# Prompt attention: the causal mask of the diagonal blocks added in PSUM by VectorE instead of by products of the unit matrix

## What the kernel computes

```python
qf = q_b.astype(f32) * (HEAD_DIM ** -0.5)
m_s = (kpos <= pos[None, None, :, None, None])          # causal
p_s = jax.nn.softmax(jnp.where(m_s, s_s, NEG_INF), axis=-1)
o_s = jnp.einsum('nhgqkl,nhqkld->nqhgd', p_s, v_g)
dlt = pos[:, None] - wpos[None, :]
m_w = (dlt >= 0) & (dlt < WINDOW) & (wpos[None, :] >= 0)  # causal for 512 rows
p_w = jax.nn.softmax(jnp.where(m_w, s_w, NEG_INF), axis=-1)
return g_b[..., 0:1] * o_c + g_b[..., 1:2] * o_s + g_b[..., 2:3] * o_w
```

## Time and profile before

| what | value |
|---|---|
| time, median of 3 runs | 797.34 us (795.62 to 798.36) |
| span of the profiled execution, first to last instruction | 795.5 us |
| TensorE busy | 762.2 us (96%) |
| VectorE busy | 379.9 us (48%) |
| ScalarE busy | 204.9 us (26%) |
| GpSimd busy | 106.8 us (13%) |
| prompt attention, about 292 to 404 us of the span | 14% of the span |

### The profile page before, as it was taken

The page is one execution under the profiler, slowest core; times in us unless marked ns, Lnnn a source line. Parts: engine busy times, 40 slices in busy tenths (PEclk is TensorE's granted clock), DMA queues, the critical chain, the costliest instruction groups (busy, mean ns, idle before and its releaser), DMA issues.

```text
span 795.5 us, 12983 instructions
## 1 busy us (share of the span) xinstructions
PE 762.2 (96%) x5070; PEld 494.9 (62%) x5070; DVE 379.9 (48%) x850; ACT 204.9 (26%) x485; POOL 106.8 (13%) x160
## 2 busy tenths in 40 slices
PE   8999999999999999889999999999999999998995
PEld 5455588777778788555566775445556564654442
DVE  3269523997232323766624378434732212214865
ACT  3011213112223354654523200134111111123223
POOL 3000006000000311334500100011111101015002
PEclk9999999999999999999999999999999999999998
DMA  9640493841440499200030279003799999996002
GB/s 324 160 126 0 112 278 139 99 133 57 140 97 17 139 233 266 94 1 1 1 120 2 96 216 384 1 14 128 282 407 409 416 418 416 417 373 211 17 14 106
DMA packets 81287, 136.50 MB, mean 172 GB/s; under 512 B 33926, under 2 KB 57546, under 8 KB 77010
## 3 DMA queue, kind: packets, MB, share of 16 engines
q1 hardware_dynamic: 64700, 110.17, 41.7%
q0 software_dynamic: 3728, 13.38, 4.9%
q10 hardware_dynamic: 12798, 12.12, 4.6%
HBM read 116.55 MB, written 21.19 MB: 173 GB/s over the span
## 4 chain that ended last, share of the span: by engine, by line
PE 80%; DMA 8%; DVE 6%; issue 2%; ACT 2%; POOL 1%; DVEq 0%; SPq 0%; POOLq 0%; ACTq 0%
PE ps L1215 29%; PE ps L1300 10%; PE ps L1656 6%; PE ps L1904 5%; PE ps L1788 4%; PE ps L1222 3%; PE ps L1776 3%; DMA merged<-in_w_exp_down 3%; DMA w_slot<-in_w_exp_down 2%; PE ps L1441 2%; PE ps L1820 2%; PE ps L1491 2%; PE ps L1537 2%; PE ps L1518 2%; DMA wgu<-expert_rows,pos_i 1%
## 5 line engine op out<-in xcount | busy, mean ns | idle before, releaser
L1215 PE MATMUL ps<-w_slot,hT 128*128 128x396 f32 (+1 forms) x192 | 71.1, 529 | 0.6 <-DMA w_slot<-in_w_in 0.4
L1215 PE MATMUL ps<-hT,w_slot 128*128 128x288 f32 x256 | 63.1, 407 | 0.0
L1215 PEld LDWEIGHTS ps<-hT,w_slot 128*128 128x128 f32 x256 | 48.3, 190 | 13.9 <-issue 0.8
L1215 PEld LDWEIGHTS ps<-w_slot,hT 128*128 128x128 f32 x192 | 36.1, 190 | 32.5 <-issue 13.4
L2987 DVE SCALAR_TENSOR_TENSOR th<-th,ps 128x256 f32<-128x256 f32 x12 | 5.1, 421 | 103.2 <-ACT th L2248 103.2
L1788 PE MATMUL ps<-w_slot,hT 128*32 128x256 f32 x544 | 49.7, 380 | 0.0
L1300 PE MATMUL ps<-hT,w_slot 128*128 128x288 f32 x144 | 37.3, 407 | 0.0
L1215 PE MATMUL ps<-qg,w_slot 128*128 128x288 f32 x128 | 33.7, 408 | 0.0
L1788 PEld LDWEIGHTS ps<-w_slot,hT 128*32 128x32 f32 x544 | 26.3, 110 | 10.0 <-issue 2.3
L2728 DVE TENSOR_REDUCE nm_p<-ps 128x2 f32<-128x256 f32 (+3 forms) x32 | 25.0, 819 | 15.6 <-PE ps L1491 15.5
L1300 PEld LDWEIGHTS ps<-hT,w_slot 128*128 128x128 f32 x144 | 27.3, 190 | 7.6 <-issue 0.2
(11 more groups left out here) (508 smaller groups left out, 1416.5 us busy)
## 6 DMA issues: line engine op xcount, KB each, us to landing
merged<-in_w_exp_down SPq DMA_DIRECT2D x10, 1024.0 KB, 15.9
w_slot<-in_w_in SPq DMA_DIRECT2D x8, 1024.0 KB, 7.7
wgu<-in_w_exp_gate SPq DMA_DIRECT2D x8, 1024.0 KB, 12.1
wgu<-in_w_exp_up SPq DMA_DIRECT2D x8, 1024.0 KB, 14.1
w_slot<-in_w_exp_gate SPq DMA_DIRECT2D x8, 1024.0 KB
w_slot<-in_w_exp_up SPq DMA_DIRECT2D x8, 1024.0 KB
w_slot<-in_w_exp_down SPq DMA_DIRECT2D x6, 1024.0 KB
expert_rows<-onsaT ACTq DMA_DIRECT2D x12, 512.0 KB, 8.2
```

The lines of the kernel that those rows point to most:

```text
L1215: ins = pe.matmul(out, a, b, start=(n == 0), stop=(n == len(pairs) - 1))
```

## The change

The 64 mask products go. The scores are written with `start=True`, and no longer wait for the mask. In their place VectorE adds `causal`, spread over the two banks of a pair, to the last 128 columns of both banks, in PSUM, and the reduction waits for that sum. The wait for the constants moves from TensorE to VectorE. The loop on TensorE is now one loop over the pairs, so that each pair's scores stand behind their own wait only.

```diff
                 if what == "s" and i == 0:
                     pe.wait_ge(*emptied(("ktn",)))
-                    pe.wait_ge(consts, 2)
...
                         if at >= 2:
                             pe.wait_ge(pr_exp, at - 1)
                         for kh in range(NKV):
-                            pe.matmul(ps[:, 2 * (at % 2) + kh, n - P:n], ident_b[:], causal[:], start=True, stop=False,
-                                      skip_group_check=True)
-                    for k in range(2):
-                        at = SLOT_OF["s", i, k]
-                        for kh in range(NKV):
                             lo = HD * kh
                             ins = pe.matmul(ps[:, 2 * (at % 2) + kh, 0:n], qT[lo:lo + HD, 2 * half + k, P * b:P * b + P],
-                                            kt[lo:lo + HD, r - 1, 0:n], start=False, stop=True, skip_group_check=True)
+                                            kt[lo:lo + HD, r - 1, 0:n], start=True, stop=True)
                         ins.then_inc(pr_scores, 1)
...
+            dve.wait_ge(consts, 2)
             dve.wait_ge(gs_ld, 16 * 16)
...
                         dve.wait_ge(pr_scores, at + 1)
+                        own = ps[:, 2 * (at % 2):2 * (at % 2) + 2, n - P:n]
+                        link(tt(own, own, causal[:].unsqueeze(1).broadcast_to([P, 2, P]), ALU.add))
                         dve.tensor_reduce(nm_p[:, at], ps[:, 2 * (at % 2):2 * (at % 2) + 2, 0:n], axis=X, op=ALU.max, negate=True
                                           ).then_inc(pr_max, 1)
```

## The result

The changed kernel takes 803.7 us (median of 6 runs, 801.57 to 804.68); the kernel before, run beside it, takes 798.22 us (6 runs). The ratio is 1.0074 with a 95% interval of 1.0055 to 1.0094: slower, and 1.1 us beyond the upper end of the range. The profiled execution has a span of 801.8 us against 795.5.

A forecast was written before the change was run, and what follows sets the result against it. TensorE was taken to set the pace in the prompt's attention, held by VectorE's copies; after a reset at u11, sums less masks in u12 to u15 add 1.81 us: 797.34 + 1.8 = 799.1 us, range 796.4 to 802.6.

The forecast's parts named there:

- TensorE's clock: Rival: longer gaps in u12 to u15 bring two more falls to 1.2 GHz, giving 801.3 us; chance 0.12.
- u11's gap: In u11 the first pair's scores run while the second pair waits for `pc`, bringing the lag back to about 0.
- the walk: Unit-by-unit tally through the prompt's attention, u0 to u15, of masks saved and sums added; ends 1.81 us slower.
- u12 to u15: Last four units: sums ahead of awaited copies, less masks saved, add 1.81 us that stays to the end.
- lag: Time after minus time before at the same place in the kernel; positive means the changed kernel is later.
- u11 resets: At u11 the +1.3 us from u10 is forgotten, as only the second pair still waits; lag about 0.
- the moved wait doesn't reset: Rival: u11's first pair can't use the gap, so +1.3 us is carried on, giving 800.4 us; chance 0.18.
- Masks in u0 to u3: First four units: TensorE has no gaps and sums find VectorE idle; four mask blocks save 1.3 us.
- u4 to u10: Sums delay copies TensorE awaits in u4, u7, u8, u9 by 0.9 us each; lag +1.3 at u10's `cs`.
- The sum's price: Each VectorE sum into PSUM lasts 0.42 us and costs 0.45, two per unit, 14.4 us in all.
- The sums are hidden: Rival: VectorE's idle time absorbs the sums and TensorE gains 16 x 0.33 = 5.3 us, giving 792.0; chance 0.13.
- What costs nothing: Free: moved wait for constants, `start=True`, and ScalarE's exponentials starting 0.45 us later, thanks to its idle room.

The follow-up runs named there:

- the two runs above: Small products filling TensorE's waits: in the changed kernel (u4, u8, u10, u11) 798.98 us; in the kernel before (u10, u11) 795.08 us.
- the kernel without sums: Changed kernel with the 32 VectorE mask sums left out, so diagonal blocks get no causal mask: 792.51 us, ratio 0.992 to the kernel before.
- the run with it alone: Kernel before with only TensorE's loop changed to one per pair, masks still products: 798.37 us, ratio 0.9991.
- sums and masks: Kernel before with VectorE's sums added and the mask products kept, in the old order: 807.71 us, ratio 1.0109.
- the copy between the pairs and the clock kept in u10 and u11: Changed kernel, VectorE's awaited copy before the second sum and maximum, small products in TensorE's waits of u10 and u11: 797.77 us, ratio 1.0003.
- the copy between the pairs alone: Changed kernel with VectorE taking the copy TensorE awaits between a unit's first and second sum and maximum: 797.95 us, ratio 1.0009.

## Why the prediction was wrong in size

The direction of the forecast held, and so did its mechanism on VectorE; its size, 1.8 us, was under a third of what came, because the sum had TensorE's clock at nothing and u11's gap too large. The 5.96 us are made up of the 1.81 of the walk, 0.85 that u11 didn't forget, 0.54 that u12 to u15 cost more, and 2.76 of clock. The table has the lag at the walk's places: as forecast, as it came, and with the clock kept in both kernels (the two runs above).

| place | forecast | after - before | clock kept in both |
|---|---|---|---|
| u5's first score | -0.7 | +1.90 | -0.12 |
| u8's first score | -0.6 | +2.00 | -0.01 |
| u10's first score | +0.9 | +4.91 | +1.33 |
| `cs` in u10 | +1.3 | +5.42 | +1.83 |
| u12's first score | 0 | +3.63 | +0.85 |
| end of the stage | +1.8 | +5.96 | +3.20 |

(Forecasts at scores are the walk's value at the copy before them less the 0.33 of the mask between.)

- **The failed step: TensorE's clock.** I priced it as a rival, with falls in u12 to u15, where the waits came out at 0.88 to 1.15 us and the clock stayed at 1.00; the sum had it at nothing. It fell in u4 and u8, for which I did not ask. In u8 the fall begins as the wait of 2.05 us ends, which my own walk had made longer by two sums. In u4 it begins ahead of the wait of 2.15 us, behind 0.46 and 0.94 us, and the kernel without sums falls there too: that wait of 0.94 us comes of the moved wait (0.58 in the run with it alone) and of the masks taken away, which the walk booked as a gain only. What the falls cost is shown by the small products: 2.03 us in u4, 1.56 more by u10's scores, and 1.59 for the one fall of the kernel before, where I had 1.1 for one. Together with what they do to u11 it is 2.76 us net of the fall that the kernel before has. Why the clock falls at one wait and not at another stays open. TensorE: Matmul & The Clock Gate of the Trainium skill (Part 1), which I cited and set aside because the stage's mean was 0.99, was the better guide: u4 and u8 agree with it that waiting costs clock, though u12 to u15 show waits that cost none.
- **u11 resets: wrong.** "The lag is back to about 0" did not come, with or without falls of the clock. The first pair does go ahead of `pc`, but the gap that it fills is worth a limited time: 1.79 us of 5.42 came back, and of 1.83 with the clock kept 0.98. That the moved wait doesn't reset was a rival; it was half right.
- **Masks in u0 to u3: mis-sized.** u4's first turn starts 22.35 us into the stage (315.00), before 23.09 (315.49): 0.74 us for four blocks, not 1.3. The kernel without sums stands at the same place at u4's scores, so it isn't the sums. The traces have the parts. Behind a run of sixteen compression products a mask starts 2.30 us after the run's start (292.40 to 294.70) and a score without a mask 2.39 us (292.65 to 295.04), so of the 0.31 us from mask to score 0.09 is lost again, and each of the four blocks gives 0.21 to 0.23 us. In u13 both start 1.01 us after the value products begin, and all of the 0.33 is won. Once, at 304.14 us, TensorE waits 0.19 us longer for VectorE to empty a bank of the compression products. Why a score starts later than a mask behind the one kind of products and not behind the other wasn't tried. The lack of 0.56 is what the last column of the table shows up to u10.
- **u4 to u10: right.** The waits in u7, u8 and u9 grew by 0.94, 1.20 and 0.94 us (0.9 forecast), that of `cs` by 0.50 (0.45).
- **u12 to u15: right, a little small.** From u12's scores to the end 2.33 us were lost, 1.81 forecast; u13 and u15 cost 0.59 and 0.93 (0.57 and 0.90 forecast), u12 0.66 in place of 0.41 and u14 0.15 in place of -0.07. The slack that I read there (0.16 and 0.2) was not to be had.
- **The sum's price: right.** 0.425 us, and 0.46 to 0.47 to the reduction behind it.
- **The sums are hidden: wrong**, by 9.5 us of the 14.4. **What costs nothing**: ScalarE's later exponentials cost nothing as long as VectorE's copies were last; once these are out of the way, ScalarE's copies take their place.

## What to carry to other kernels

An engine that is half idle on average can still have no slack on one path: ask what stands behind the new operation in its queue, and put what another engine awaits ahead of it. When a change lengthens TensorE's waits, look at every place with such a wait, the early ones too, and price the products behind it at the lower clock; work taken off TensorE lengthens its waits as well, as in u4. Some small products in the wait can be cheaper than the fall. And where a wait seems to absorb a lag, count how much it can absorb.

## What the runs showed of the hardware

- The granted clock fell at different points about TensorE's waits: as one of 2.05 us ended (changed kernel, u8); some 1.5 us after the end of one of 2.22 us (sums and masks, u4); within one of 1.29 us, behind 0.46 and 0.95 (no sums, u4); and behind 0.46 and 0.94 or 0.95 us alone, before the next wait (u4 of the changed kernel, and of the one with the copy between the pairs and the clock kept in u10 and u11). Behind 0.46 and 0.95 us it stayed at 1.00 in the kernel with the copy between the pairs alone, as it did about waits of 0.88 to 1.15 us in u12 to u15 and of 1.78 us in u8 with sums and masks. What decides it is left open. TensorE: Matmul & The Clock Gate of the Trainium skill (Part 1) says that the point at which the clock rises varies from run to run; for the fall, the two kernels with the copy between the pairs, whose programs are the same up to that place, show as much.
- Executions of one kernel differ in it. Of 23 of the kernel before, the fastest (795.15 us) has a mean granted clock of 0.996 over the span and the slowest (802.33 us) 0.987. So the falls of one profile are those of one execution.
- Small products that compute nothing kept the clock at 1.00 in every stretch where they filled a wait. With nothing else altered the kernel before gets 0.3% faster by them (0.1 to 0.5%), and the changed kernel goes from a ratio of 1.0074 to 1.0024.
- A sum of 256 columns into PSUM takes 0.425 us, the same as the 0.42 of one out of PSUM.
